# A hybrid decoder layer: second projection weight block loaded before the later rows of x, and the first two projections taken group by group

## The reference, cut to what matters

```python
def rmsnorm(x, g):
    out = xf * lax.rsqrt(jnp.mean(xf * xf, axis=-1, keepdims=True) + NORM_EPS) * g
z = jnp.einsum('btd,de->bte', rmsnorm(x, ln), w_in)      # one combined projection
u, q, k, v, qi, ki, wi = [z[..., offs[i]:offs[i + 1]] for i in range(len(IN_SPLITS))]
s = jnp.einsum('bqhd,bld->bqhl', qi, ki_all) * (IDX_DIM ** -0.5)
score = jnp.einsum('bqhl,bqh->bql', jax.nn.relu(s), wi) * (IDX_HEADS ** -0.5)
_, idx = lax.top_k(score, topk)
```

## Time and profile before

| | |
|---|---|
| median of 3 runs | 1374.95 us (1371.79 to 1374.96) |
| profiled execution | 1372.92 us, its span 1371.1 us |
| TensorE busy | 1314.8 us (96%) |
| VectorE, ScalarE, GpSimd busy | 51%, 39%, 44% |
| HBM | 101 GB/s over the span |

### The profile page before, as it was taken

The page is one execution under the profiler, slowest core; times in us unless marked ns, Lnnn a source line. Parts: engine busy times, 40 slices in busy tenths (PEclk is TensorE's granted clock), DMA queues, the critical chain, the costliest instruction groups (busy, mean ns, idle before and its releaser), DMA issues.

```text
span 1371.1 us, 25240 instructions
## 1 busy us (share of the span) xinstructions
PE 1314.8 (96%) x9720; PEld 1216.8 (89%) x9720; DVE 702.3 (51%) x1611; ACT 531.2 (39%) x1071; POOL 600.6 (44%) x610
## 2 busy tenths in 40 slices
PE   4989999999999999998899999999899999999998
PEld 4958999995566899777899999999899999999997
DVE  6368997768875222236924434434543333333445
ACT  5345887737777222234433333333301110111034
POOL 5333974342440311221377667667333333333610
PEclk9999999998999999999999999999999999999999
DMA  6330123310001876872233323323522331232203
GB/s 196 83 90 16 47 55 111 91 35 1 1 11 38 285 232 191 260 235 80 79 110 118 109 88 126 102 87 126 189 81 76 110 110 58 99 107 103 69 4 127
DMA packets 143549, 141.68 MB, mean 103 GB/s; under 512 B 21080, under 2 KB 111320, under 8 KB 143423
## 3 DMA queue, kind: packets, MB, share of 16 engines
q1 hardware_dynamic: 124933, 116.31, 26.7%
q10 hardware_dynamic: 17842, 21.94, 4.4%
q0 software_dynamic: 656, 1.84, 0.6%
HBM read 111.87 MB, written 26.50 MB: 101 GB/s over the span
## 4 chain that ended last, share of the span: by engine, by line
PE 80%; DVE 6%; ACT 2%; issue 2%; POOL 1%; DVEq 0%; ACTq 0%; POOLq 0%
PE bank L2066 73%; PE bank L2242 2%; PE bank L2304 2%; DVE junk L1643 1%; ACT sjunk L1112 1%; PE bank L2383 1%; PE bank L2112 1%; POOL rdenb L848 1%; DVE lack L1647 1%; DVE hn_lo L1867 1%; DVE hid_lo L1990 1%; PE bank L2556 0%; DVE sqacc L1854 0%; PE bank L2268 0%; DVE prob L1734 0%
## 5 line engine op out<-in xcount | busy, mean ns | idle before, releaser
L2066 PE MATMUL bank<-hid_hi,w_hi 128*128 128x384 f32 (+1 forms) x672 | 218.8, 326 | 4.9 <-DVE hid_lo L1990 4.9
L2066 PE MATMUL bank<-hid_lo,w_hi 128*128 128x384 f32 (+1 forms) x672 | 217.9, 324 | 0.0
L2066 PE MATMUL bank<-hid_hi,w_lo 128*128 128x384 f32 (+1 forms) x672 | 217.0, 323 | 0.0
L2023 DVE TENSOR_TENSOR acc<-bank,acc 128x384 f32<-128x384 f32 x168 | 87.7, 523 | 205.1 <-PE bank L2066 205.1
L897 POOL TENSOR_TENSOR w_hi<-w_raw,zero 128x1024 fp32r<-128x1024 f32 x32 | 62.0, 1939 | 246.6 <-PE bank L2066 228.6
L686 POOL TENSOR_TENSOR w_hi<-w_raw,zero 128x256 fp32r<-128x256 f32 x108 | 69.0, 639 | 204.5 <-PE bank L2066 188.9
L2066 PE MATMUL bank<-xn_hi,w_hi 128*128 128x384 f32 (+1 forms) x456 | 150.7, 330 | 2.9 <-POOL w_lo L688 2.1
L2066 PE MATMUL bank<-xn_lo,w_hi 128*128 128x384 f32 (+1 forms) x456 | 147.3, 323 | 0.0
L2066 PE MATMUL bank<-xn_hi,w_lo 128*128 128x384 f32 (+1 forms) x456 | 146.9, 322 | 0.0
L1394 ACT ACTIVATE hid_hi<-hraw 128x1056 fp32r<-128x1056 f32 x32 | 32.7, 1077 | 256.6 <-PE bank L2066 167.3
L2066 PEld LDWEIGHTS bank<-hid_hi,w_hi 128*128 128x128 f32 x672 | 127.0, 189 | 5.1 <-DVE hid_lo L1990 5.1
(11 more groups left out here) (298 smaller groups left out, 3222.9 us busy)
## 6 DMA issues: line engine op xcount, KB each, us to landing
w_raw<-in_w_ff_dram SPq DMA_DIRECT2D x50, 512.0 KB, 3.4
hraw<-hidden_dram SPq DMA_DIRECT2D x16, 1056.0 KB, 7.2
page<-in_cache_k_dram SPq DMA_DIRECT2D x64, 256.0 KB, 3.9
page<-in_cache_v_dram SPq DMA_DIRECT2D x64, 256.0 KB, 3.4
hidden_dram<-stg ACTq DMA_DIRECT2D x56, 264.0 KB, 2.1
w_raw<-in_w_in_dram SPq DMA_DIRECT2D x18, 512.0 KB, 3.6
wr<-in_w_ff_dram SPq DMA_DIRECT2D x14, 512.0 KB, 4.5
xrow<-in_x_prompt_dram SPq DMA_DIRECT2D x8, 512.0 KB, 8.1
```

Source lines behind the costliest of these rows:

```text
L2023: nc.vector.tensor_tensor(v, ps[:, 0:w], v, ALU.add).then_inc(freeof(("dn", gi, m, g)), 1)
L2066: return nc.tensor.matmul(out, lhsT, rhs, start=start, stop=stop)
```

## The change

Block 1's load is issued right behind block 0's, in front of rows 3 to 8 of x. The six tiles of blocks 0 and 1 are taken group by group: both blocks for group 0, then both for group 1, then both for group 2. ScalarE copies out the third tile between `high(1)` and `high(2)`.

```diff
-        head_tiles = [(0, 0), (1, 0), (0, 1), (0, 2), (1, 1), (1, 2)]
+        head_tiles = [(0, 0), (1, 0), (0, 1), (1, 1), (0, 2), (1, 2)]
...
             for t in range(3):
                 x_rows(t)
             w_load(sp, 0)
+            w_load(sp, 1)
             for t in range(3, NT):
                 x_rows(t)
-            w_load(sp, 1)
             sp.dma_start(hist[:, :], state_pool[0].rearrange("b t c -> (b t) c")).then_inc(s_hl, 16)
...
             head_out(0)
             head_out(1)
             high(1)
+            head_out(2)
             high(2)
-            for q in range(2, 6):
+            for q in range(3, 6):
                 head_out(q)
```

## The result

The changed kernel took 1376.75 us (median of 20 executions, 1375.42 to 1381.41), the kernel before 1374.11 us beside it (20 executions, 1371.17 to 1376.12). The ratio is 1.0023, with a 95% interval from 1.0016 to 1.0030: 2.6 us later in the medians and 3.2 by the ratio. That is a small but real loss, since the interval lies wholly above 1, and it is inside the 0.3% that the prediction set for "same". The prediction said 1376.0 us, 2.05 later. The profiled execution took 1375.72 us with a span of 1373.9, 2.8 later than before.

The account below looks back on a forecast made before the run. TensorE, busy 1314.8 of 1371.1 us, was taken as the bound. 2.45 - 0.4 = 2.05 us later gave 1375.0 from the profiled execution and 1377.0 from the median; the middle, 1376.0, was predicted, range 1371.8 to 1379.8.

Parts of the forecast that it names:

- same: Whole kernel: a time within about 0.3% (4.1 us) of before, 1370.8 to 1379.1 us; chance 0.85.
- Term 2: Before block 2: POOL's split waits for block 0's buffers, a new TensorE stall of 2.45 us (bounds 2.3 and 3.7).
- Nothing covers it: At the 2.45 us stall before block 2: TensorE has no other work in its order, POOL no other way.
- Term 1: At block 1's first tile: weight wait exchanged for a row wait, 0.4 us earlier (bounds 1.7 earlier, 0.2 later).
- rival 2: First tile after the stand in `norm_T(0)` runs at 1.2 GHz: 4.1 us more, 1380.1 us; chance 0.10.
- So I take 0.1: First tile after the stand in `norm_T(0)`: slow clock costs 0.1 us, with bounds of nothing and 4.2 us.
- Rival 3: SP's queue: tile 3's issue held until DMA engines run dry, `low(0)` slips, 2.1 us more, 1378.1; chance 0.08.
- Rival 4: Load of block 1: DMA engines mix transfers, it lands no earlier, term 1 zero, 2.45 later, 1376.4; chance 0.05.
- Rival 1: Search stage: TensorE's 1.9 us wait for ScalarE's copy can vanish and swallow the shift, 1374.1 us; chance 0.18.
- Rival 5: Whole kernel: a real gain, 2.1 us at most, needing term 2 absent; gains by luck fall under other outcomes, 0.04.

Follow-up runs that it names:

- e3: The changed kernel with a high and a low buffer of its own for block 2's split; 1372.77 us, ratio 0.9998 to the kernel before.
- e2: The changed kernel with block 1's load back behind the rows, so the new order of tiles alone; 1375.83 us, ratio 1.0016 to the kernel before.
- e11: The kernel of e2 run again for a second profile; 1376.06 us, ratio 1.0027 to the kernel before.
- e1: The kernel before with block 1's load moved in front of rows 3 to 8, old order of tiles; 1373.68 us, ratio 1.0004.
- e4: The changed kernel with 18 transposes of the identity filling the stall in front of block 2; 1378.80 us, ratio 1.0034 to the kernel before.
- e9: The changed kernel run again for a second profile; 1377.58 us, ratio 1.0037 to the kernel before.
- e10: The changed kernel with 12 matmuls, result unused, filling the stall in front of block 2; 1377.21 us, ratio 1.0035 to the kernel before.
- e5: The kernel before, old order of tiles, with block 1's load between row tiles 5 and 6; 1371.37 us, ratio 0.9989.
- e6: The changed kernel with block 1's load between row tiles 5 and 6 and own buffers for block 2; 1371.46 us, ratio 0.9993 to the kernel before.
- e7: The kernel of e1 with 80 transposes of the identity ahead of `norm_T(0)`; 1372.72 us, ratio 1.0000 to the kernel before.

## Why the prediction was right

**Term 2 held.** Predicted 5.99 - 3.54 = 2.45 us in front of block 2; the three profiles in which the clock stays give 2.47 to 2.50. That POOL's wait for block 0's buffers causes it is shown by e3: with other buffers the stall is gone, and the ratio is 0.9998. That the order is its cause is shown by e2 and e11, which hold the order alone (1.0016 and 1.0027), and by e1, which has the load's move without it (1.0004).

**What follows term 2 was missing.** "Nothing covers it" was right, but the sum ended there. In three of the four profiles with the stall left open the clock fell behind it (not in e2), and 1.5 us more went into slow matmuls. The prediction asked about the clock only for the stand in `norm_T(0)`, and set it aside there with one row ("the 2.10 us stall at 24.2 did not slow what followed"); e11 shows a stand of 1.85 us at the same place that did. One profiled execution can't tell that a stand is free. The two fillers were to show what share of the median this has, and they don't. The profiled executions of both were their fastest, with the highest mean clock (0.991), and most of the others lost several us somewhere that no profile shows. That stays open.

**Term 1 was right in its steps and wrong in its sum.** The steps of the rows: a block costs those behind it 1.54 us by the prediction, 1.30 by tile 5 (14.71 - 13.41) and 1.68 by two blocks together. One reading in it is loose: the 1.28 us between tiles 3 and 5 are ScalarE's own pace, since no wait for a DMA stands in front of tiles 4 and 5. The bytes give nearly the same, 1.24 to 1.27 us for a row tile of 512 KB (an estimate from the 414 to 422 GB/s of the windows from 12 to 14 us before), so the term stands. `low(0)` starts at 18.19 against 18.5 predicted. POOL goes from block 0 to block 1 without a gap, as it said, and the stall at block 1 is gone.

Block 1's tile came at 25.05 in the profile of the change, 0.85 earlier than the 25.9 predicted, because `low(0)` was 0.3 early and the second half of `norm_T(0)` ran at full pace from 18.87. But that was one execution. Six profiles have the load in front of all later rows and no filler ahead of the head: the change, e1, e3, e4, e9 and e10. Their `norm_T(1)` is -1.35, +1.54, +0.71, +0.32, +0.86 and -0.09 against before, a mean of 0.33 us later where 0.4 earlier was predicted, and four of the six lie beyond the term's bound of 0.2 later, which had left the clock to rival 2. The rows are not what is off: the first tile starts at 21.58 on average, with 21.5 as the middle predicted. It is the tile's length, 5.15 us on average (4.30 to 5.87) where 4.3 and 0.1 for the clock were predicted. So the step that failed is "So I take 0.1" for the clock, which measured 0.85.

**Rival 2 is real, below its full price.** Its mechanism, the first tile at the pace of 1.2 GHz behind a stand in `norm_T(0)`, appears in four of the six profiles with 4 to 10 of the 24 matmuls slow (e1, e3, e4, e9) and hardly in the other two (none and two). Its price was set too high: a slow matmul costs 0.145 us more, not 0.175, so that a wholly slow tile would cost 3.5 us instead of 4.2. The point from which it was to decide, 13 of 24 (15 by the measured price), was not reached in any profile. The old wait for block 1's weights hid this: in e2 two slow matmuls moved nothing.

**The other rivals.** Rival 3's row appeared without its harm. The five issues of row tiles 3 to 7 took 5.67 us, of which the first, tile 3's, held SP for 3.75; before, SP stood 5.41 us on the history's one. But the DMA engines never ran dry: their share is 0.99 or more in each window of 1 us from 3 to 16 us.

```profile
2.15 1.54 SPq L517 DMA_DIRECT2D w_raw<-in_w_in_dram  x2
3.73 5.67 SPq L537 DMA_DIRECT2D xrow<-in_x_prompt_dram  x5
...
9.91 0.48 SPq L545 DMA_DIRECT2D hist<-in_state_pool_dram  x1
```

Rival 4 is refuted by the rows of POOL and tile 5 at 14.71. Rival 1 was not seen: the wait of 1.9 us is there in the profile of the change and block 3 starts 2.54 us later, against 2.67 for `klow`. Rival 5 was right that no gain is in this form. The gain that exists, 1.5 to 1.7 us, lies in another place for the load (e5), which the prediction didn't look for: it keeps the rows in time and removes the wait for block 1.

**The sum.** 2.05 us were predicted, 2.64 measured in the medians (3.2 by the ratio) and 4.5 in e9. The parts, by the profiles, are 2.5 for the stall and 0.3 for the head, 2.8 together, and 4.3 in the executions in which the clock falls behind the stall. So both misses, 0.7 us in term 1 and 1.5 at times behind term 2, have one sign, and the forecast was a little low. The interval of e9, 1.0021 to 1.0052, reaches over the mark of 0.3%; the 20 executions with 1.0023 decide for "same", by little. Some luck is in how near 1376.0 came to 1376.75. It was the middle of two sums and stood only 1.05 us above 1374.95, the median of three runs; with 20 the kernel before has 1374.11, and the loss is larger. In the profile of the change, too, two misses cancel in part: term 1 came 0.95 us better than predicted, and the clock behind the stall took 1.5.

## What to carry to other kernels

A load moved forward in a queue delays every load that it passes: before moving it to the front, find the last place at which it is still in time (here three row tiles later, 0.9989 instead of 1.0004). A change in the order of tiles also changes when double buffers come free; count the work that is left between the last reader of a buffer and the first reader of what replaces it, and set it against the refill (here 3.54 us against 5.99). And a short stand of TensorE has two prices, the stand and the matmuls behind it, of which the second varies between executions of one kernel; one profile of it is not enough.

## What the runs showed that was not expected

**The clock goes with much of the kernel's scatter.** Each execution has a mean granted clock beside its time. Over the 35 executions of the kernel before beside e1 to e4 a straight line through the two has a correlation of -0.92, with 0.91 us less for each 0.001 of clock; the clocks go from 0.985 to 0.991. On such lines, taken at a clock of 0.988, the kernel before stands at 1373.7, e1 at 1374.2, e3 at 1373.7, e2 at 1376.1 and e4 at 1378.1. So e4's loss is not one of the mean clock, and it is the part that stays open. The changed kernel stands at 1376.9 in its first 20 executions and at 1376.7 in e9 (1374.0 for the kernel before beside e9), so the gap between its two ratios, 1.0023 and 1.0037, goes for the most part with the clock. Which of the two is cause isn't shown by a line: the falls behind stands are themselves part of the mean.

**A stand of 1.4 to 2.2 us can lower the clock and need not.** It did behind the stand at block 2 in the change, e9 and e11, and behind the one at block 1 in e11, for ten or eleven matmuls each time; it didn't at block 2 in e2, nor at block 1 in the profile of before. A shorter one stands in the score stage of every profile: TensorE waits 1.40 us for VectorE's `score` before its last two matmuls with `kst`. In e1, e2 and e6 the clock falls to 0.50 within 1.3 us of its end, and these are the three in which block 3 comes 1.4 to 1.7 us later than `klow` says. The row of the change, where it stays up, and that of e1:

```profile
108.59 0.73 PE L2067 MATMUL bank<-kst,qst 128*128 128x512 f32 x2 [1.40 <-DVE score L1587]
```

```profile
107.53 1.22 PE L2066 MATMUL bank<-kst,qst 128*128 128x512 f32 x2 [1.40 <-DVE score L1586]
```

**The record of the granted clock reads 1.00 where the pace is that of 1.2 GHz.** In e1 the matmuls from 22.5 to 25.4 us start 0.32 us apart, and the windows read full clock:

```profile
22.00:24.00 2.00, 2.00 (x8) 2.00 (x8) 1.96 (x4) 1.94 (x5) 0.05 (x1) 1.00 0.16 36
24.00:26.00 2.00, 2.00 (x9) 2.00 (x8) 1.66 (x3) 2.00 (x5) 0.00 (x0) 1.00 0.21 47
```

In e7, where the clock had risen before, the same pace reads 0.50. At the start of a kernel the distance between matmuls is what to go by, not the column of the clock.
